# Attention two heads a step, with score products in the two row halves of the array

## The reference

```python
qa = rotary(...); ka = rotary(...)      # group A: 8 query heads, 2 key/value heads, 64 wide
sc = einsum(qc, chunk_band(k, 2)) * 64 ** -0.5        # A: own and previous chunk of 64 tokens
m = maximum(max(sc), sink); p = exp(sc - m); p = p / (sum(p) + exp(sink - m)); o = p @ v
sc = einsum(qc, chunk_band(k, 9)) * 64 ** -0.5 + bias  # B: 8 heads, own and 8 previous chunks
p = softmax(sc); o = p @ v
x = x + concat(rmsnorm(oa), rmsnorm(ob)) @ w_out
```

## Time and profile before

| | us |
|---|---|
| median of 3 runs | 2818.72 |
| the runs | 2818.07 to 2822.78 |
| span of the profiled execution | 2815.7 |
| attention within it, first score product to last value product | 537.1 to 911.9 |

### The profile page before, as it was taken

One profiled execution on the slowest core, in us unless ns is written; L12 is line 12 of the kernel. 1 busy time (PEld: TensorE's weight loads), 2 busy tenths in 40 slices (PEclk: granted clock), 3 DMA queues, 4 the chain that ended last, 5 costly groups with the idle time before them and its releaser, 6 DMA issues.

```text
span 2815.7 us, 39454 instructions
## 1 busy us (share of the span) xinstructions
PE 2767.0 (98%) x14294; PEld 2347.4 (83%) x14294; DVE 1583.8 (56%) x2721; ACT 1064.3 (38%) x2101; POOL 1066.7 (38%) x754
## 2 busy tenths in 40 slices
PE   9999999999999999999998999999999999999998
PEld 9888888899999787888886888888888887888876
DVE  3355664666688332333336766668766666654354
ACT  6433333466666221333324333334333333222342
POOL 7645454210000111321215654555654553552152
PEclk9999999999999999999999999999999999999999
DMA  8657768656664534122226332335423335644454
GB/s 279 241 183 249 261 206 268 199 145 160 164 141 111 183 126 177 51 90 79 66 73 224 108 100 89 112 113 187 127 97 97 102 113 194 234 141 142 141 175 136
DMA packets 244600, 428.48 MB, mean 152 GB/s; under 512 B 17857, under 2 KB 151489, under 8 KB 239169
## 3 DMA queue, kind: packets, MB, share of 16 engines
q1 hardware_dynamic: 207008, 358.43, 40.1%
q10 hardware_dynamic: 37408, 67.65, 7.5%
HBM read 285.50 MB, written 135.27 MB: 149 GB/s over the span
## 4 chain that ended last, share of the span: by engine, by line
PE 55%; DVE 2%; DMA 1%; POOL 1%; ACT 1%; issue 0%; SPq 0%; POOLq 0%; ACTq 0%; DVEq 0%
PE gu_acc L51 9%; PE gu_acc L53 9%; PE gu_acc L52 9%; PE down_acc L51 4%; PE down_acc L52 4%; PE down_acc L53 4%; PE cross_sum_o L51 2%; PE cross_sum_s L51 2%; PE cross_sum_s L53 2%; PE cross_sum_o L53 2%; PE cross_sum_o L52 2%; PE cross_sum_s L52 2%; DVE gu_t L2493 0%; PE cross_turned L2171 0%; PE cross_turned L1889 0%
## 5 line engine op out<-in xcount | busy, mean ns | idle before, releaser
L51 PE MATMUL gu_acc<-gu_t,shared_m 128*128 128x512 f32 x704 | 275.0, 391 | 4.3 <-DVE gu_t L2493 4.3
L53 PE MATMUL gu_acc<-gu_t,shared_m 128*128 128x512 f32 x704 | 274.6, 390 | 0.0
L52 PE MATMUL gu_acc<-gu_t,shared_m 128*128 128x512 f32 x704 | 274.6, 390 | 0.0
L350 POOL TENSOR_TENSOR front_wq_lo<-front_wq_raw,front_wq_hi 128x1024 fp32r<-128x1024 f32 x72 | 179.0, 2487 | 203.9 <-ACT front_wq_hi L346 203.7
L2436 ACT ACTIVATE shared_m<-kept_x 128x512 fp32r<-128x512 f32 x175 | 109.3, 628 | 210.0 <-PE gu_acc L53 188.1
L51 PEld LDWEIGHTS gu_acc<-gu_t,shared_m 128*128 128x128 f32 x704 | 132.6, 188 | 34.0 <-issue 4.1
L53 PEld LDWEIGHTS gu_acc<-gu_t,shared_m 128*128 128x128 f32 x704 | 132.5, 188 | 27.5
L52 PEld LDWEIGHTS gu_acc<-gu_t,shared_m 128*128 128x128 f32 x704 | 132.5, 188 | 27.5
L346 ACT ACTIVATE front_wq_hi<-front_wq_raw 128x1024 fp32r<-128x1024 f32 x72 | 76.1, 1058 | 188.1 <-PE qkv_acc L53 98.3
L51 PE MATMUL gu_acc<-shared_m 128*128 128x512 f32 x352 | 137.9, 392 | 2.9 <-POOL shared_m L2409 2.5
L52 PE MATMUL gu_acc<-shared_m 128*128 128x512 f32 x352 | 137.4, 390 | 0.0
(11 more groups left out here) (356 smaller groups left out, 7859.1 us busy)
## 6 DMA issues: line engine op xcount, KB each, us to landing
front_wq_raw<-in_w_in ACTq DMA_DIRECT2D x69, 512.0 KB, 3.9
ahead_w_even<-in_w_gate SPq DMA_DIRECT2D x44, 512.0 KB, 4.5
kept_x<-in_w_up SPq DMA_DIRECT2D x44, 512.0 KB, 4.3
a_d<-gu_a_mix SPq DMA_DIRECT2D x88, 256.0 KB, 3.2
a_d<-gu_a SPq DMA_DIRECT2D x66, 256.0 KB, 4.2
kept_x<-in_w_down SPq DMA_DIRECT2D x56, 256.0 KB, 4.7
shared_m<-a_d SPq DMA_DIRECT2D x19, 704.0 KB, 4.3
beside_turned<-a_d SPq DMA_DIRECT2D x19, 704.0 KB, 4.0
```

The costliest lines, as they stand in the source:

```text
L51: pe.matmul(out, l_hi, r_hi, start=first, stop=False)
L52: pe.matmul(out, l_hi, r_lo, start=False, stop=False)
L53: return pe.matmul(out, l_lo, r_hi, start=False, stop=last)
L350: pool.tensor_tensor(self.lo[:, i % Q_SLOTS, :], self.raw[:, i % Q_SLOTS, :], raw(self.hi[:, i % Q_SLOTS, :]), ALU.subtract).then_inc(self ...
```

## The change

The jobs become pairs of heads for B too: `JOBS` has 4 B pairs and 4 A pairs, 8 x 16 = 128 units, each of two heads (x = 0, 1). q and k lie as `qk_d` has them, head 0 in rows 0 to 63 and head 1 in rows 64 to 127, the high part in one tile and the low part in another, and nothing is doubled (for A the one key head is still copied to both halves). A score is three products of 64 rows (q high·k high, q high·k low, q low·k high), the two heads in turn: head 0 in the upper row half of the array, head 1 in the lower, into banks of their own. `sum_s` is now one buffer of two banks for each head, no longer two for each of two units, so `score(u)` waits for both maxima of unit u-1. Scores of A take 192 columns, not 256.

PE's order in a step is turn(s-2, head 0), score(s), turn(s-2, head 1), values(s-3). DVE's is divide(s-4), a copy, the two maxima of s, a copy. ACT does a copy and an Exp for each head. The small subtraction and addition of A go from DVE to POOL. q, k, v are loaded by quarters of a job (512 tokens) in rings of 3 (q), 4 (k, as columns of the same tile) and 4 (v); quarter Q's load is issued when quarter Q-3 is through. `stage_qkv` loads two quarters ahead rather than four pieces of one head. Two tiles move: `h1` is allocated ahead of the rows' buffers, and 88 float32 of padding stand at the right end of SBUF, so that `wout_w_hi`, `wout_w_lo` and `wout_ident` lie 352 bytes lower in each partition.

In the bytes of a partition: `h0` stays at 16512; `h1` goes from 107264 to 95872, beside `front_wq_hi`, which goes from 61568 to 66688; `wout_w_hi` goes from 187872 to 187520 beside `mix_m_hi` at 103040, which stays.

```diff
@@ -647,8 +647,8 @@
 
     with ExitStack() as ctx:
         room = Room(nc, ctx, "qkv", ends)
+        h1 = [room.sb(f"h1{part}", [P, KT, BANK], F32R) for part in range(2)]
         rows = Rows(room)
-        h1 = [room.sb(f"h1{part}", [P, KT, BANK], F32R) for part in range(2)]
         hs = (h0, h1)
         OB = 5
...
+Q_RING, V_RING = 3, 4
...
+        self.k = [flat[0][:, part * SEQ:(part + 1) * SEQ] for part in range(2)]
+        self.k_both = raw(flat[0]).rearrange("p (a t) -> p a t", a=2)
+        self.q = [[flat[1][:, (2 * r + part) * BANK:(2 * r + part + 1) * BANK] for part in range(2)]
+                  for r in range(Q_RING)]
+        self.q_both = [flat[1][:, 2 * r * BANK:2 * (r + 1) * BANK] for r in range(Q_RING)]
+        at = 2 * Q_RING * BANK
+        self.v = [raw(flat[1][:, at + r * 2 * BT * HD:at + (r + 1) * 2 * BT * HD])
+                  .rearrange("p (h t c) -> p h t c", h=2, t=BT) for r in range(2)]
+        self.bias = room.sb("bias0", [P, 2, B_WIN * P])
...
+        sp.dma_start(raw(self.q_both[z]).rearrange("p (a t) -> p a t", a=2),
+                     qk_d[:, 0, :, cols].rearrange("a p t -> p a t")).then_inc(self.s_first[z], 16)
+        sp.dma_start(self.k_both[:, :, cols], qk_d[:, 4, :, cols].rearrange("a p t -> p a t")).then_inc(self.s_first[z], 16)
+        for x in range(2):
+            sp.dma_start(self.v[z][:, x, :, :], v_d[2 + x, :, at, :]).then_inc(self.s_first[z], 16)
...
+PHASE = 88
...
+        kept.sb("pad", [P, PHASE])
...
-    JOBS = [("b", h) for h in range(8)] + [("a", pp) for pp in range(N_PAIR)]
+    JOBS = [("b", x) for x in range(N_PAIR)] + [("a", x) for x in range(N_PAIR)]
...
-        sum_s = [room.bank(f"sum_s{j}", 2) for j in range(2)]
+        sum_s = [room.bank(f"sum_s{x}", 2) for x in range(2)]
...
+                def load(Q):
+                    J, z = divmod(Q, N_BLK)
                     kind, x = JOBS[J]
-                    rows = slice(part * HD, (part + 1) * HD)
-                    slots = q_slots(J)
+                    cols, at, s_in = slice(z * BANK, (z + 1) * BANK), slice(z * BT, (z + 1) * BT), s_ld[Q % 4]
+                    q_to = raw(first.q_both[Q % Q_RING]).rearrange("p (a t) -> p a t", a=2)
+                    k_to = first.k_both[:, :, cols]
+                    v_to = v_t[Q % V_RING]
+                    q_tile = x if kind == "b" else Q_UNROT + x
+                    sp.dma_start(q_to, qk_d[:, q_tile, :, cols].rearrange("a p t -> p a t")).then_inc(s_in, 16)
                     if kind == "b":
-                        sp.dma_start(raw(q_t[slots[0]][rows, cols]),
-                                     qk_d[part, x // 2, x % 2 * HD:(x % 2 + 1) * HD, cols]).then_inc(s_in, 16)
-                    elif slots == (1, 2):
-                        sp.dma_start(raw(q_more[rows, 0:2, cols]),
-                                     qk_d[part, Q_UNROT + x, :, cols].rearrange("(h r) t -> r h t", h=2)
-                                     ).then_inc(s_in, 16)
+                        sp.dma_start(k_to, qk_d[:, 4 + x, :, cols].rearrange("a p t -> p a t")).then_inc(s_in, 16)
+                        for h in range(2):
+                            sp.dma_start(v_to[:, h, :, :], v_d[2 + 2 * x + h, :, at, :]).then_inc(s_in, 16)
                     else:
-                        for y in range(2):
-                            sp.dma_start(raw(q_t[slots[y]][rows, cols]),
-                                         qk_d[part, Q_UNROT + x, y * HD:(y + 1) * HD, cols]).then_inc(s_in, 16)
-
-                def load_v(J, at, s_in):
-                    kind, x = JOBS[J]
-                    sp.dma_start(v_t[k_slot(J)][:, at, :], v_d[2 + x if kind == "b" else x // 2, :, at, :]
-                                 ).then_inc(s_in, 16)
-
-                def load(J, cols, at, s_in):
-                    for part in range(2):
-                        load_q(J, part, cols, s_in)
-                    if loads(J) == 7:
-                        load_k(sp, J, cols, s_in)
-                        load_v(J, at, s_in)
+                        head = x // 2
+                        for copy_at in (slice(0, HD), slice(HD, P)):
+                            sp.dma_start(k_to[copy_at, :, :], qk_d[:, N_QK - 1, head * HD:(head + 1) * HD, cols]
+                                         .rearrange("a p t -> p a t")).then_inc(s_in, 16)
+                        sp.dma_start(v_to[:, 0, :, :], v_d[head, :, at, :]).then_inc(s_in, 16)
...
+                for Q in range(3, N_QUARTER):
+                    sp.wait_ge(s_o, 2 * BT * (Q - 2))
+                    load(Q)
+                    if Q % 2 == 0 and Q // 2 < KT:
+                        load_w(Q // 2)
+                    if Q in (7, 11):
+                        load_bias((Q + 1) // N_BLK)
...
+                def minus_sink(u):
+                    first_head = JOBS[UNITS_ALL[u][0]][1] * 2
+                    pool.wait_ge(s_max, 2 * u + 2)
+                    after(pool, s_sink_exp, u - A0 - 3)
+                    pool.tensor_tensor(below[:, u % 4, :], top[:, u % 4, :], sink[:, first_head:first_head + 2],
+                                       ALU.subtract).then_inc(s_below, 1)
+
+                def whole_sum(u):
+                    pool.wait_ge(s_sink_exp, u - A0 + 1)
+                    after(pool, s_out, u - 3)
+                    pool.tensor_tensor(whole[:, u % 4, :], total[:, u % 4, :], sink_exp[:, u % 4, :], ALU.add
+                                       ).then_inc(s_whole, 1)
+
+                pool.wait_ge(s_sink, 1)
+                for u in range(A0, NB + 1):
+                    if u < NB:
+                        minus_sink(u)
+                    if u > A0:
+                        whole_sum(u - 1)
...
                 for step in range(NB + 2):
-                    if step >= 2:
-                        copy(act, copied, step - 2, 0)
-                    if step < NB:
-                        exps(step)
-                    if step in store_at:
-                        store(store_at[step])
-                    if step == NB - HT + 4:
+                    if 2 <= step < NB + 2:
+                        copy(act, copied, step - 2, 0, 0)
+                    if 1 <= step < NB + 1:
+                        exp(step - 1, 0)
+                    if 2 <= step < NB + 2:
+                        copy(act, copied, step - 2, 1, 0)
+                    if 1 <= step < NB + 1:
+                        exp(step - 1, 1)
+                    J, late = divmod(step, NT)
+                    if late == 7 and 1 <= J < 2 * N_PAIR:
...
+                for step in range(NB + 4):
+                    if step >= 4:
+                        divide(step - 4)
+                    if 2 <= step < NB + 2:
+                        copy(dve, dve.tensor_copy, step - 2, 0, 1)
                     if step < NB:
-                        maxima(step)
+                        maxima(step, 0)
+                        maxima(step, 1)
                     if 2 <= step < NB + 2:
-                        copy(dve, dve.tensor_copy, step - 2, 1)
+                        copy(dve, dve.tensor_copy, step - 2, 1, 1)
                     if step == 3:
                         stored(dve)
-                    if step >= 3:
-                        divide(step - 3)
                 norm.start_dve(dve)
                 norm.dve_scale(dve, 0, 0)
...
+                    Q = quarter(u)
+                    if i % BT == 0:
+                        if Q < 2:
+                            pe.wait_ge(s_first[Q], LOADS * 16)
+                        else:
+                            pe.wait_ge(s_ld[Q % 4], loaded[Q])
+                    w, end = width(u), (i + 1) * P
+                    halves = [(0, w, 0)] if w <= BANK else [(0, w // 2, 0), (w // 2, w, BANK)]
+                    for x in range(2):
+                        after(pe, s_max, 2 * (u - 1) + x + 1)
+                    for a, b, bank in halves:
+                        for n, (qp, kp) in enumerate(((0, 0), (0, 1), (1, 0))):
+                            for x in range(2):
+                                rows = slice(x * HD, (x + 1) * HD)
+                                last = pe.matmul(sum_s[x][:, bank:bank + b - a],
+                                                 first.q[Q % Q_RING][qp][rows, i % BT * P:(i % BT + 1) * P],
+                                                 first.k[kp][rows, end - w + a:end - w + b],
+                                                 start=n == 0, stop=n == 2)
+                                if n == 2 and b == w:
+                                    last.then_inc(s_s, 1)
...
                 for step in range(NB + 3):
+                    if 2 <= step < NB + 2:
+                        turn(step - 2, 0)
                     if step < NB:
                         score(step)
                     if 2 <= step < NB + 2:
-                        turn(step - 2)
-                    if step >= 3:
+                        turn(step - 2, 1)
+                    if 3 <= step < NB + 3:
```

(13 more changed lines are left out.)

282 lines of the change are left out of this document (104 added, 178 removed).

## The result

The changed kernel takes 2831.65 us (median of 4 runs, 2830.60 to 2832.32), the kernel before beside it 2819.47: a ratio of 1.0036, 95% interval 1.0023 to 1.0049, so 0.36% slower. A second set of runs of the same kernel gave 1.0040 (1.0026 to 1.0053). I had forecast 2789, faster. The profiled execution of the changed kernel has a span of 2828.8 us, 13.1 more than before.

The account below looks back on a forecast made before the run. PE was taken to bound the kernel, alone in B and with DVE close behind in A. Terms -32.1 + 9.0 - 1.5 + 3 - 8 = -29.6 gave span 2786.1, time 2789; likeliest range 2775 to 2805, all 2774 to 2840.

Parts of the forecast that it names:

- the one on crossings: PE in attention: 256 changes between 128 and 64 rows; way back 0.07 us in each of 128 steps, +9.0 us.
- my first rival: PE's array runs empty at each crossing, 0.27 us each: +9 becomes +60, time 2840; chance 0.15 near full price.
- shows nothing beyond the slots: Argument against the empty array: on PE, going from scores to transpositions shows no time beyond the slots.
- Pairs, -32.1: Attention's score products on PE: two heads' 64-row products run beside each other, saving 32.1 us in B and A.
- serial loads: Rival for score products: weight loads go one after another, -32.1 becomes +10.7, time 2832; chance 0.14.
- nothing side by side: Rival for score products: neither products nor weight loads overlap, +40.5 us, time 2862; chance 0.04.
- DVE to POOL, -1.5: A part: two small operations leave DVE for POOL, and PE loses 1.5 us of its idle time.
- Single score buffer, +3: Attention: scores wait for both maxima of the unit before; covered in full B steps, +3 us where jobs start.
- Loads, 0: Attention's q, k, v loads by quarters arrive in time: 0 us counted, 0 to 16 possible.
- Two addresses, -8: Products from h1 and in mix: operands a multiple of 512 bytes apart take 0.2267 us each, -8 us.
- last rival at 2862: Score products: nothing runs side by side, neither products nor weight loads; time 2862, chance 0.04.
- What I named as signs: PE's timeline: paired starts, group about 0.97 us, B steps 4.2 to 4.3; gaps over 0.1 us mean drain.

Follow-up runs that it names:

- full_rows: Changed kernel with score products over all 128 rows, two per head and half instead of three of 64 rows; 2814.90 us, ratio 0.9977 to the kernel before.
- before_in_new_order: Kernel before with the two addresses moved and PE's order as in the changed kernel, all products over 128 rows; 2815.70 us, ratio 0.9979.
- changed_2: The changed kernel once more, unaltered, run for comparison beside others; 2831.45 us, ratio 1.0040 to the kernel before.
- addresses: Kernel before with the two addresses moved alone, attention as it was; 2813.22 us, ratio 0.9970.
- two_A_units: Changed kernel with the A part's score products of two units in one group of 12; 2827.78 us, ratio 1.0023 to the kernel before.
- both_heads_in_one_half: Changed kernel with all 12 score products in rows 0 to 63, head 1 reading head 0's rows; 3267.89 us, ratio 1.1584 to the kernel before.

## Why the prediction was wrong, point by point

The step that failed is the one on crossings: for the way back to 128 rows I took 0.07 us as the nearest row (+9.0), where the two crossings of a step cost 0.34 to 0.35 beyond entering the group. 128 steps make 44 us and not 9. That is nearly the mechanism of my first rival (the weight load can't go ahead, the array runs empty). Counted as that rival counts, with the 0.07 of entering the group in it, a crossing is (44 + 9) / 256 = 0.21 us where the rival had 0.27, just where it said that it decides: by this term alone the forecast of 2789 becomes 2824. The rival's chance of 0.15 was too small. The Trainium skill's rule that a change of tiling mode drains TensorE (page "TensorEngine Tiling (Array Packing)", section "Key Properties") agrees with the weight loads here: the first one of the new mode starts 0.20 us after the last product of the old one has started, and 0.002 where the mode stays. Against it I had set that going from scores to transpositions "shows nothing beyond the slots", a row with 128 rows on both sides, which says nothing of a change of mode.

The other terms, from the trace of the changed kernel:

- *Pairs, -32.1.* Right. A B group has six slots of 0.148 (from 12 in 1.08 and 8 in 1.26), an A group three of 0.11. The rivals of serial loads and of nothing side by side are out.
- *DVE to POOL, -1.5.* Too small. full_rows takes 1.71 for an A step against 1.87 before; 0.055 of it are the 192 columns. The remaining 0.10 is DVE's (before_in_new_order has none of it): 60 x 0.10 = -6. I had looked for DVE's part in PE's idle time, where it does not show. In B full rows take 4.45, where 4.50 less the one entry of 0.07 that the sum saves is 4.43: 48 x 0.02 = +1.
- *Single score buffer, +3.* PE waits 5.1 us, 4.2 more than before, at the job starts as foreseen. But only 1.3 of it, where attention starts, are waits for the maxima; 3.3 are waits for DVE's copy.
- *Loads, 0.* Right.
- *Two addresses, -8.* The size was right (-8.4 alone), and the sign came: the slots from h1 are 0.227 us by the median and those in mix too. But in the profiled execution `stage_qkv` is only 2.7 us shorter and mix only 1.2, together 4.1 less than the 8. The granted clock was at half there for 3.4 us in each (114 to 120 us: 0.72; 950 to 957 us: 0.76), and in the trace of before in neither. In changed_2's trace, which has neither of the two, the stages are 3.3 and 2.8 us shorter.
- *Not foreseen: the clock at the start.* At the start of attention, where PE waits between short steps, the clock is granted at half for longer in the changed kernel's trace than in that of before. The window 542 to 546 us in the kernel before and then in the changed one:

```profile
542.00:546.00 4.00, 4.00 (x36) 3.98 (x35) 3.66 (x14) 3.24 (x8) 0.00 (x0) 1.00 1.02 221
```

```profile
542.00:546.00 4.00, 4.00 (x23) 3.14 (x21) 2.17 (x8) 1.95 (x6) 0.00 (x0) 0.51 1.02 409
```

From 534 to 546 us the missing share of the clock sums to 1.7 us before and 5.1 after: +3.4. How much of this is the change's own is open. The clock is at half there for 3.4 us before and 10.2 after, but for 6.8 us in changed_2, which is the changed kernel, in `addresses`, whose attention is that of before, too, and for 17.1 us in two_A_units, whose B part is that of the changed kernel.

The sum again: forecast -29.6, measured +13.1, 42.7 apart. Crossings +35, clock +3.4, waits +1.2, addresses +4.1, DVE's part in A -6 + 1.5, full B steps +1, together 40. About 2 more lie outside attention, `stage_qkv` and mix; what is left is under 1 us. Two smaller things in the prediction's numbers: the 3.0 us between span and median mixed two executions (for single runs the record has 1.8 between span and time), and the range of all, 2774 to 2840, left out its own last rival at 2862.

What I named as signs was right: a gap of more than 0.1 us on both sides of the group came, the B step was not 4.2 to 4.3, the pairs were there, and the group took 1.08, not 0.97: about 0.11 of the crossings' price lies inside the group, 0.03 in the first slot and 0.09 between the last product and the transposition behind it.

## What to carry to other kernels

Before small products are packed into parts of the array, count how often the array changes between whole and parts: here one change there and back costs 0.35 us, and a pair, three of which stand in place of four products over all rows, saves 0.05 us (320 columns) or 0.04 (192), so that it takes 7 or 10 pairs between two changes to break even, and there were 6 and 3. A price for an operation of a new kind must not be taken from transitions between operations of the old kind; when a rule says that they differ, give it more weight than a row that can't speak to it. And an engine can hold PE by less than a record's overlap on every unit without ever appearing among PE's waits: compare slots, start to start, with those of the same group elsewhere.

## What the runs showed of the hardware

- A change from 128-row to 64-row products and back costs 0.34 to 0.38 us, about 0.20 on the way in and 0.15 on the way back. On the way in the new weight load starts 0.20 us after the start of the last 128-row product, and not 0.002. The borders are there too when the other row half is not used at all (both_heads_in_one_half, at half clock: 0.13 and 0.05 us beyond the slots of the transpositions).
- Products in different row halves run beside each other, weight loads too, even when three products of one half stand ahead of the other half's in order (starts 10 ns apart).
- With 64-row products in one half only, the granted clock stayed at 0.50 for some 820 us in which PE was busy without a break, and rose to 1.00 at about 1365 us, in the run of 30 transpositions of 128 rows behind the last value products; with the other half filled beside it, the changed kernel was back at full clock by about 546 us. Why is not shown.
- With one operand a whole multiple of 512 bytes from the other in every partition a 512-column product takes 0.2267 us, and not 0.2324 (89.25 times 512) or 0.2333 (165.69 times). Why, and whether 256 would do, is not shown.
- The same kernel is granted half the clock for 6.8 us in one execution and 10.2 in another at the same place (changed_2 and the changed kernel).
- A score product behind a transposition starts 0.03 us after it, behind a value product 0.08 (medians of before_in_new_order and before), and a full B unit takes 2.21 us and not 2.25.
